# Two transformer blocks on one core: products of constants between a norm and its first matmuls

## The chip, the cores and the metric

The kernel runs on one core of a Trainium2 chip. A core has five engines, each with its own instruction queue: TensorE (PE) multiplies 128x128 tiles and writes PSUM, VectorE (DVE), ScalarE (ACT) and GpSimd (POOL) do the rest of the arithmetic, and SyncE (SP) issues most of the DMAs. They meet through semaphores. The metric is the device time of one execution in microseconds. The kernel before takes 2858.25 us, the median of 3 runs (2855.25 to 2858.81).

## The reference, cut to what matters

The reference is two layers of a first kind of block (differential attention, then neighbourhood attention, each with a squared-relu MLP and modulated norms), followed by two blocks of a second kind, and a last norm. There are 256 latent and 256 context tokens, of 1024 features.

```python
def rms_norm(x, g):
    xf = x.astype(jnp.float32)
    y = xf * lax.rsqrt(jnp.mean(xf * xf, axis=-1, keepdims=True) + NORM_EPS)
    return (y * g.astype(jnp.float32)).astype(x.dtype)
...
    for i in range(DEPTH):
        mod_l = jnp.split((jax.nn.silu(c) @ w_mod[i] + b_mod[i])[:, None, :], N_MOD, axis=-1)
        h_l = modulate(rms_norm(x, norm1_g[i]), mod_l[0], mod_l[1])
        ...
        x = x + mod_l[2] * y_l
        x = x + mod_l[5] * squared_relu_mlp(modulate(rms_norm(x, norm2_g[i]), mod_l[3], mod_l[4]),
                                            w_mlp1[i], w_mlp2[i])
...
    for l in range(DEPTH):
        x = x + HALF_STEP * swiglu(rms_norm_2(x, ffn1_norm[l]), ffn1_w_gu[l], ffn1_w_down[l])
        x = x + hybrid_mixer(rms_norm_2(x, mix_norm[l]), positions, ...)
        x = x + memory_cross_attention(rms_norm_2(x, ca_norm[l]), rms_norm_2(mem, mem_norm[l]), ca_w_q[l], ca_w_kv[l], ca_w_o[l])
        x = x + HALF_STEP * swiglu(rms_norm_2(x, ffn2_norm[l]), ffn2_w_gu[l], ffn2_w_down[l])
    return rms_norm_2(x, final_norm)
```

All of it is float32. The added products compute nothing of this: their results are not read.

## The kernel before, in words

**Layout.** The residual stream `XT` is held transposed, eight tiles of 128 features by 512 tokens (256 of the context, 256 latents); in the second kind of block, and in the last MLP, only the 256 latent columns count. Weights come by DMA in blocks of up to 1 MB into a ring of three slots. ScalarE makes the rounded copy `Wh` (L1249) and VectorE the remainder `Wl` (L1689); activations are split the same way into `HTh` and `HTl`. `passes` (L685) multiplies such a pair in three passes, each a matmul of one record in the trace. Two split blocks of weights are held at a time.

**A norm.** ScalarE squares the tiles of `XT` into `Pb` and `Lb`. `norm` (L768) lets TensorE multiply the eight squares by a tile of ones, in plain f32, all into one PSUM bank, so that each token's sum stands in every partition. ScalarE makes the inverse root of it (L1280 to L1283), VectorE one Newton step (L1747 to L1749), and then tile by tile VectorE scales (`TMP`, L1760 or L1782), ScalarE rounds (`HTh`) and VectorE takes the remainder (`HTl`, L1767 or L1696). Each `HTl` raises `lo_ready`.

**The first matmuls behind a norm.** `side_by_side` (L739) fills two banks at once, tile by tile, waiting for `lo_ready` at each of the eight tiles. That is a group of 8 x 2 x 3 = 48 matmuls. TensorE has nothing else to do between the norm's last product and the first `HTl`. The last norm, `fin`, is followed by 16 transposes of `HTf`, four into each of four banks, which ScalarE copies out (L1312) for the output's DMA.

**Modulation.** In layer 0, the rows of the modulation are made on TensorE from weights as they land (L800), copied to `modrow`, and 16 products with the constant `fold` (two columns each) turn them into columns. The norm `n1` of layer 0 is issued ahead of the last rows.

**Memory attention.** `attention` (L839) is a loop over units. In step i it issues the scores of unit i, what `behind` gives, the transposes of unit i-2 and the product with the values of unit i-3. For the memory attention, `behind(1)` (in step 2) issues the last 48 matmuls of the queries, and `behind(2)` waits for their copy.

**PSUM and order.** Eight banks of 128x512 f32 are two pools of four, `A` and `V`, each taken in turn. A bank is taken again when the fourth taker before is done with it (`a_free`, `v_free`). The order of each engine's instructions is the order in which its function is written; no scheduler moves anything.

Of the kernel before, what the change touches and what calls it, by code (L numbers as in the profile page):

```python
# [28 lines left out]
P = 128  # L29
# [4 lines left out]
LAT = slice(S, 2 * S)  # L34
ALL = slice(0, 2 * S)
# [38 lines left out]
BANKS = 4  # L74
# [188 lines left out]
def program(nc, I, out):  # L263
    ctx = ExitStack()
    with ctx:

        start = (nc.sbuf_base + 31) // 32 * 32
# [7 lines left out]
        def place(name, shape, dt=F32):  # L275
            t = over(name, shape, here[0], dt)
            here[0] += (4 * int(np.prod(shape[1:])) + 31) // 32 * 32
            assert here[0] <= start + ARENA, name
            return t
# [3 lines left out]
        def sem(name):  # L283
            sems[name] = ctx.enter_context(nc.semaphore(name))
            return sems[name]
# [15 lines left out]
        con = place("con", [P, PACK.shape[1]])  # L301
# [30 lines left out]
        def squares(k):  # L332

            return Pb[:, k, :] if k < 6 else Lb[:, k - 6, :]

        def C(name):
            a, n = CONST[name]
            return con[:, a:a + n]
# [69 lines left out]
        v_full, v_free = sem("v_full"), sem("v_free")  # L408
        A, V = Pool(pa, a_full, a_free), Pool(pv, v_full, v_free)
# [238 lines left out]
        def _(pe):  # L648
# [3 lines left out]
            def mm(o, lhsT, rhs, start, stop, full=None):  # L652
                m = nc.tensor.matmul(o, lhsT=lhsT, rhs=rhs, start=start, stop=stop)  # L653
                if full is not None:
                    m.then_inc(full, 1)

            def turn(o, x, full=None):
                m = nc.tensor.transpose(o, x, C("ident"))  # L658
                if full is not None:
                    m.then_inc(full, 1)  # L660
# [42 lines left out]
            def group(pool, key, o, pairs):  # L703

                if pool.taken():
                    pe.wait_ge(pool.free, pool.taken())
                bank = pool.take(key)
                for i, (a, b, ready) in enumerate(pairs):
                    if ready is not None:
                        ready()  # L710
                    last = i == len(pairs) - 1
                    mm(o(bank), a, b, i == 0, last, pool.full if last else None)
# [52 lines left out]
            X_TOKS = [(X_AT, t) for t in range(2)]  # L765
            CTX_TOKS = [slice(t * P, (t + 1) * P) for t in range(2)]

            def norm(key, tcols):  # L768
                N = tcols.stop - tcols.start
                group(A, key, lambda b: b[:, 0:N],  # L770
                      [(C("ones")[:, 0:P], squares(k)[:, 0:N], lambda: pe.wait_ge(sq_ready, seen.more(sq_ready)))
                       for k in range(KT)])

            def turn_in(key, tok, tiles):
                for k in range(KT):
                    if V.taken():
                        pe.wait_ge(v_free, V.taken())
                    b = V.take((key, k))
                    for t in range(tiles):
                        turn(b[:, t * P:(t + 1) * P], tok[:, t, k * P:(k + 1) * P], v_full if t == tiles - 1 else None)  # L780

            def turn_rows(key, rows):

                if V.taken():
                    pe.wait_ge(v_free, V.taken())
                n = rows.shape[0]
                m = nc.tensor.transpose(V.take(key)[:, 0:n], rows, C("ident")[0:n, 0:n])
                m.then_inc(v_full, 1)

            def condition_rows(pool, key):  # L790

                w = raw_slot()
                if pool.taken():
                    pe.wait_ge(pool.free, pool.taken())
                b = pool.take(key)
                for k in range(KT):
                    j = k % 4
                    m = nc.tensor.matmul(b[32 * j:32 * j + 32, 0:256], lhsT=cT[:, k, :], rhs=w[:, k, :],  # L800
                                         start=k < 4, stop=k >= 4)
                m.then_inc(pool.full, 1)
                used(pool, key)

            def modulation(i):
                pe.wait_ge(v_free, V.nth("cond"))
                for n in range(FIRST_MOD):
                    condition_rows(V, ("modr", i, n))
                    if n == X_AFTER:
                        pe.wait_ge(const_in, 16)  # L810
                        pe.wait_ge(rows_in, ROW_LOADS * 16)
                        for j in range(2):
                            turn_rows(("rows", j), rowt[0:min(P, N_ROWS - j * P), j, :])
                        pe.wait_ge(tok_in, 4 * 16)
                        turn_in("x", xtok, 4)
                    if n == X_AFTER + 3:
                        norm(("n1", i), ALL)
                if V.taken():
                    pe.wait_ge(v_free, V.taken())
                b = V.take(("mod", i))  # L820
                pe.wait_ge(v_free, V.nth(("modr", i, FIRST_MOD - 1)))
                for n in range(2 * KT):
                    mm(b[:, 2 * n:2 * n + 2], modrow[:, n // 2, n % 2 * P:n % 2 * P + P], C("fold"), True, True,
                       v_full if n == 2 * KT - 1 else None)

            def next_modulation(n):

# [11 lines left out]
            def attention(tag, kind, todo, scores, values, dv, o_rows, also=lambda i: None, behind=lambda i: None):  # L839


                for i in range(len(todo) + 3):
                    if i < len(todo):
                        for m in range(2 if kind == "diff" else 1):
                            pairs = scores(*todo[i], m)
                            if V.taken():
                                pe.wait_ge(v_free, V.taken())
                            b = V.take((tag, "S", i, m))
                            for j, (q, k, *where) in enumerate(pairs):
                                last = j == len(pairs) - 1  # L850
                                mm(b[:, where[0] if where else slice(0, todo[i][2])], q, k, j == 0, last,
                                   v_full if last else None)
                    if i:
                        behind(i - 1)
                    if 0 <= i - 2 < len(todo):
                        u = i - 2
                        n = todo[u][2] // P
                        pe.wait_ge(pn_ready, seen.more(pn_ready))
                        if A.taken():
                            pe.wait_ge(a_free, A.taken())  # L860
                        b = A.take((tag, "T", u))
                        src = Pb[:, u % 3 * 2, :]
                        for t in range(n):
                            turn(b[:, t * P:(t + 1) * P], src[:, t * P:(t + 1) * P], a_full if t == n - 1 else None)
                    if i >= 3:
                        u = i - 3
                        h, qt, nk = todo[u]
                        pe.wait_ge(a_free, A.nth((tag, "T", u)))
                        r = o_rows(h)
                        group(V, (tag, "O", u), lambda b: b[r, 0:P],  # L870
                              [(values(h, t), PT[:, u % 2, t * P:(t + 1) * P], None) for t in range(nk // P)])
                    also(i)
                behind(len(todo) + 2)
# [40 lines left out]
            def first_layer(i):  # L914
                if i == 0:
                    modulation(0)
                else:
                    norm(("n1", i), ALL)
                tiles = qk_tiles(i)
                order = len(tiles)  # L920
                for j in range(order + 2):
                    if j < order:
# [4 lines left out]
                        n = c.stop - c.start  # L927
# [10 lines left out]
                    if 0 <= j - 1 < order:  # L938
                        c = tiles[j - 1][1]
                        n = c.stop - c.start  # L940
# [13 lines left out]
                if i == 0:  # L954
# [18 lines left out]
                    N, tc = 512, ALL  # L973
                    src = ht(ALL)
                else:
# [4 lines left out]
                    N, tc = S, LAT  # L980
                    src = quarters(lambda k: O_AT["near"] + k)
                for n in range(4):
                    linear(V, ("o", i), 2 * n, (0, P), src, N, n == 0 and i == 0)
                norm(("n2", i), tc)
                for c in range(FF1 // P // CHUNK + 1):
                    if i == DEPTH - 1 and c == MEMORY_CHUNK:
                        pe.wait_ge(mem_in, 16)
# [62 lines left out]
                group(V, (tag, j, "r"), lambda b: b[:, 0:S], [(C("halves"), x, None)])  # L1050

            def mixer(l):
                norm(("mix", l), LAT)
                for n in range(3):
                    linear(A, ("fqk", l), 2 * n, (0, P), hx, S, n == 0)
                section_values(("fv", l))
# [17 lines left out]
                for j, offsets in enumerate(((0, P), (0, HEAD), (0, P))):  # L1074
                    linear(A, (("sb", l), "qk"), 2 * j, offsets, hx, S)
                    if j == 0:
# [3 lines left out]
                        b = V.take(("cum", l))  # L1080
# [121 lines left out]
            for i in range(DEPTH):  # L1202
                first_layer(i)
            for l in range(DEPTH):
# [1 line left out]
                mixer(l)  # L1206
                cross(l)
                ffn(l, 2)
            norm(("fin",), LAT)
            pe.wait_ge(h_ready, seen.more(h_ready, KT))  # L1210
            for t in range(2):
                for half in range(2):
                    if A.taken():
                        pe.wait_ge(a_free, A.taken())
                    b = A.take(("out", t, half))
# [1106 lines left out]
```

## Time and profile before

| | us |
|---|---|
| median of 3 runs | 2858.25 |
| lowest, highest | 2855.25, 2858.81 |
| the profiled execution | 2857.25 |
| its span (first to last instruction) | 2855.4 |
| TensorE busy | 2686.0 |
| VectorE busy | 1726.7 |
| ScalarE busy | 1283.4 |

Times come from one profiled execution. "PE" rows are matmuls and transposes, "PEld" their weight loads, which run beside them. A duration of a matmul's record holds its drain, so consecutive records overlap; the pace is the distance of two starts. The granted clock is the share of TensorE's full 2.4 GHz; it has two levels, 0.5 and 1, and a value between is a mean over a stretch. A wait in square brackets is the idle time of the engine before that instruction, with what ended it. "issue" there means that the profile shows nothing that it waited for.

### The profile page before, as it was taken

What the parts mean: (1) busy time and instruction counts of PE and PEld (TensorE: products, weight loads), DVE (VectorE), ACT (ScalarE), POOL (GpSimd) and SP (SyncE); (2) the same over time, 40 slices, a digit from 0 to 9 for tenths busy, and PEclk for the clock granted to TensorE, in tenths of its full rate; (3) what the DMA queues carried; (4) which work ended last, traced back from release to release, by engine and by line L of the source; (5) the groups of instructions that cost most, each with busy time, mean ns of one, the idle gap of its engine ahead of it and who ended that gap; (6) DMA issues with size and microseconds to landing.
All of it is one profiled execution on the core that took longest, in us unless ns stands there. A gap on an engine that the chain in (4) does not pass through costs nothing.

```text
span 2855.4 us, 45577 instructions
## 1 busy us (share of the span) xinstructions
PE 2686.0 (94%) x18789; PEld 2397.7 (84%) x18789; DVE 1726.7 (60%) x3256; ACT 1283.4 (45%) x2348; POOL 129.6 (5%) x146
## 2 busy tenths in 40 slices
PE   5999989999979889999989989899999999898998
PEld 3777567888868589999989879899999998798998
DVE  4554855454565566676555767676665447675763
ACT  3544733223254554454443445554544434455543
POOL 1000000000040410000000020000000000110000
PEclk9999999999989899999999999999999999999999
DMA  7555532323252335556544314365665543243654
GB/s 246 192 177 172 169 103 74 104 91 101 99 108 76 73 96 172 163 173 181 167 154 139 117 52 159 115 177 163 192 182 168 168 142 111 67 141 119 175 165 119
DMA packets 511518, 397.09 MB, mean 139 GB/s; under 512 B 21848, under 2 KB 487008, under 8 KB 511184
## 3 DMA queue, kind: packets, MB, share of 16 engines
q1 hardware_dynamic: 508512, 387.10, 44.7%
q0 software_dynamic: 2080, 3.53, 1.0%
q8 instruction: 150, 2.46, 0.4%
q10 hardware_dynamic: 720, 3.54, 0.3%
q14 instruction: 56, 0.46, 0.1%
HBM read 393.08 MB, written 1.05 MB: 138 GB/s over the span
## 4 chain that ended last, share of the span: by engine, by line
PE 83%; DVE 9%; ACT 4%; issue 1%; DMA 1%; POOL 1%; SPq 0%; DVEq 0%; ACTq 0%
PE pv L688 42%; PE pa L688 31%; PE pv L653 5%; PE pa L653 3%; DVE Wl L1689 2%; ACT Wh L1249 2%; PE pa L658 1%; PE pa L800 1%; DMA ring<-in_w_mod_dram 1%; DVE Lb L1827 1%; POOL Pb L2244 0%; DVE TMP L1782 0%; DVE T L1748 0%; DVE TMP L1760 0%; DVE HTl L1767 0%
## 5 line engine op out<-in xcount | busy, mean ns | idle before, releaser
L1689 DVE TENSOR_TENSOR Wl<-ring,Wh 128x1024 fp32r<-128x1024 f32 (+3 forms) x688 | 765.2, 1153 | 351.3 <-ACT Wh L1249 348.7
L1249 ACT ACTIVATE Wh<-ring 128x1024 fp32r<-128x1024 f32 (+3 forms) x688 | 647.4, 990 | 504.9 <-PE pv L688 502.0
L688 PE MATMUL pa<-HTl,Wh 128*128 128x256 f32 (+1 forms) x1648 | 539.5, 327 | 43.9 <-DVE HTl L1767 26.9
L688 PE MATMUL pv<-HTl,Wh 128*128 128x256 f32 (+1 forms) x1872 | 545.9, 292 | 9.1 <-DVE XT L1807 2.2
L688 PE MATMUL pv<-HTh,Wl 128*128 128x256 f32 (+1 forms) x1872 | 537.0, 287 | 0.0
L688 PE MATMUL pv<-HTh,Wh 128*128 128x256 f32 (+1 forms) x1872 | 536.6, 287 | 0.0
L688 PE MATMUL pa<-HTh,Wl 128*128 128x256 f32 (+1 forms) x1648 | 524.1, 318 | 0.0
L688 PE MATMUL pa<-HTh,Wh 128*128 128x256 f32 (+1 forms) x1648 | 523.7, 318 | 0.0
L688 PEld LDWEIGHTS pa<-HTl,Wh 128*128 128x128 f32 x1648 | 324.2, 197 | 79.8 <-issue 43.3
L688 PEld LDWEIGHTS pv<-HTl,Wh 128*128 128x128 f32 x1872 | 358.9, 192 | 22.5 <-issue 7.4
L688 PEld LDWEIGHTS pv<-HTh,Wl 128*128 128x128 f32 x1872 | 359.2, 192 | 3.2 <-issue 0.5
L688 PEld LDWEIGHTS pv<-HTh,Wh 128*128 128x128 f32 x1872 | 359.1, 192 | 2.7
L688 PEld LDWEIGHTS pa<-HTh,Wl 128*128 128x128 f32 x1648 | 324.5, 197 | 19.7 <-issue 1.4
L688 PEld LDWEIGHTS pa<-HTh,Wh 128*128 128x128 f32 x1648 | 323.7, 196 | 18.5
L1312 ACT ACTIVATE BIG<-pa 128x256 f32<-128x256 f32 (+1 forms) x206 | 78.7, 387 | 331.3 <-PE pa L688 323.4
L688 PE MATMUL pv<-HID2l,Wh 128*128 128x256 f32 x704 | 199.2, 283 | 0.0
L688 PE MATMUL pv<-HID2h,Wl 128*128 128x256 f32 x704 | 199.2, 283 | 0.0
L688 PE MATMUL pv<-HID2h,Wh 128*128 128x256 f32 x704 | 199.2, 283 | 0.0
L688 PE MATMUL pv<-HID1l,Wh 128*128 128x512 f32 (+1 forms) x512 | 172.0, 336 | 0.0
L688 PE MATMUL pv<-HID1h,Wl 128*128 128x512 f32 (+1 forms) x512 | 172.0, 336 | 0.0
L688 PE MATMUL pv<-HID1h,Wh 128*128 128x512 f32 (+1 forms) x512 | 172.0, 336 | 0.0
L1797 DVE SCALAR_TENSOR_TENSOR XT<-pv,MOD,XT 128x256 f32<-128x256 f32 x216 | 95.6, 479 | 114.9 <-PE pv L688 114.1
(223 smaller groups left out, 4052.4 us busy)
## 6 DMA issues: line engine op xcount, KB each, us to landing
ring<-in_ffn_w_gu_dram SPq DMA_DIRECT2D x176, 512.0 KB, 5.0
ring<-in_w_mlp_dram SPq DMA_DIRECT2D x64, 1024.0 KB, 5.3
ring<-in_w_in_dram SPq DMA_DIRECT2D x54, 1024.0 KB, 5.1
ring<-in_w_mod_dram SPq DMA_DIRECT2D x48, 1024.0 KB, 5.6
ring<-in_ffn_w_down_dram SPq DMA_DIRECT2D x64, 704.0 KB, 4.5
ring<-in_a_w_qkv_dram SPq DMA_DIRECT2D x12, 1024.0 KB, 5.2
ring<-in_b_w_qkv_dram SPq DMA_DIRECT2D x12, 1024.0 KB, 5.2
ring<-in_w_out_dram SPq DMA_DIRECT2D x8, 1024.0 KB, 5.0
```

What stands on the lines that cost most here:

```text
L653: m = nc.tensor.matmul(o, lhsT=lhsT, rhs=rhs, start=start, stop=stop)
L658: m = nc.tensor.transpose(o, x, C("ident"))
L688: m = nc.tensor.matmul(o, lhsT=x, rhs=y, start=first and j == 0, stop=last and j == 2)
L800: m = nc.tensor.matmul(b[32 * j:32 * j + 32, 0:256], lhsT=cT[:, k, :], rhs=w[:, k, :], start=k < 4, stop=k >= 4)
L1249: ins = nc.scalar.activation(Wh[rows, p % SPLIT, a:b], ring[rows, i % RING, a:b], ACT.Copy)
L1312: nc.scalar.activation(dst, src(b), func, scale=scale).then_inc(a_free, 1)
L1689: ins = v.tensor_tensor(Wl[rows, p % SPLIT, a:b], ring[rows, i % RING, a:b], Wh[rows, p % SPLIT, a:b].bitcast(F32), ALU.subtract)
L1797: m = v.scalar_tensor_tensor(XT[:, k, half], b[:, at:at + S], MOD[:, i, gate * KT + k, w:w + 1], XT[:, k, half], ALU.mult, ALU.add)
L1827: v.tensor_tensor_reduce(Lb[:, i % 2 * 2 + m, 0:n], b[:, 0:n], mask(*todo[i]), -scale, -NEG, ALU.add, ALU.min, nm[:, i % 2, m:m + 1]).then ...
```

## The change

A new function `keep_busy(pool, n)` issues n plain f32 products of constants, the tile of ones by the first 512 columns of the packed constants `con`, into the bank that the pool gives next, without taking it. It waits first until that bank is free. The taker that follows writes the same bank, on the same engine. There are 92 such products: 5 ahead of the products with `fold`, 7 behind them, 15 behind the norm `n1` of layer 1, 15 and 8 behind `n2` of layers 0 and 1, 8 behind `mix` of each of the two later blocks, 7 in step 2 of each memory attention ahead of the first transposes, and 12 behind the last norm. The norms of the MLPs of the second kind (`f`), of the memory (`nm`) and `ca` get none.

```diff
--- before.py
+++ after.py
@@ -765,11 +765,23 @@
             X_TOKS = [(X_AT, t) for t in range(2)]
             CTX_TOKS = [slice(t * P, (t + 1) * P) for t in range(2)]
 
-            def norm(key, tcols):
+            def keep_busy(pool, n):
+
+
+
+                if pool.taken():
+                    pe.wait_ge(pool.free, pool.taken())
+                b = pool.banks[pool.n % BANKS]
+                for _ in range(n):
+                    nc.tensor.matmul(b[:, 0:512], lhsT=C("ones")[:, 0:P], rhs=con[:, 0:512], start=True, stop=True)
+
+            def norm(key, tcols, busy=0):
                 N = tcols.stop - tcols.start
                 group(A, key, lambda b: b[:, 0:N],
                       [(C("ones")[:, 0:P], squares(k)[:, 0:N], lambda: pe.wait_ge(sq_ready, seen.more(sq_ready)))
                        for k in range(KT)])
+                if busy:
+                    keep_busy(A, busy)
 
             def turn_in(key, tok, tiles):
                 for k in range(KT):
@@ -815,13 +827,13 @@
                         turn_in("x", xtok, 4)
                     if n == X_AFTER + 3:
                         norm(("n1", i), ALL)
-                if V.taken():
-                    pe.wait_ge(v_free, V.taken())
+                keep_busy(V, 5)
                 b = V.take(("mod", i))
                 pe.wait_ge(v_free, V.nth(("modr", i, FIRST_MOD - 1)))
                 for n in range(2 * KT):
                     mm(b[:, 2 * n:2 * n + 2], modrow[:, n // 2, n % 2 * P:n % 2 * P + P], C("fold"), True, True,
                        v_full if n == 2 * KT - 1 else None)
+                keep_busy(A, 7)
 
             def next_modulation(n):
 
@@ -852,6 +864,8 @@
                                    v_full if last else None)
                     if i:
                         behind(i - 1)
+                    if kind == "mem" and i == 2:
+                        keep_busy(A, 7)
                     if 0 <= i - 2 < len(todo):
                         u = i - 2
                         n = todo[u][2] // P
@@ -915,7 +929,7 @@
                 if i == 0:
                     modulation(0)
                 else:
-                    norm(("n1", i), ALL)
+                    norm(("n1", i), ALL, 15)
                 tiles = qk_tiles(i)
                 order = len(tiles)
                 for j in range(order + 2):
@@ -981,7 +995,7 @@
                     src = quarters(lambda k: O_AT["near"] + k)
                 for n in range(4):
                     linear(V, ("o", i), 2 * n, (0, P), src, N, n == 0 and i == 0)
-                norm(("n2", i), tc)
+                norm(("n2", i), tc, 15 if i == 0 else 8)
                 for c in range(FF1 // P // CHUNK + 1):
                     if i == DEPTH - 1 and c == MEMORY_CHUNK:
                         pe.wait_ge(mem_in, 16)
@@ -1050,7 +1064,7 @@
                 group(V, (tag, j, "r"), lambda b: b[:, 0:S], [(C("halves"), x, None)])
 
             def mixer(l):
-                norm(("mix", l), LAT)
+                norm(("mix", l), LAT, 8)
                 for n in range(3):
                     linear(A, ("fqk", l), 2 * n, (0, P), hx, S, n == 0)
                 section_values(("fv", l))
@@ -1206,7 +1220,7 @@
                 mixer(l)
                 cross(l)
                 ffn(l, 2)
-            norm(("fin",), LAT)
+            norm(("fin",), LAT, 12)
             pe.wait_ge(h_ready, seen.more(h_ready, KT))
             for t in range(2):
                 for half in range(2):
```

TensorE at the norm `n2` of layer 0: `Pb`, `Lb` are the squares, `HTl` and `HTh` the operand, `Wh` and `Wl` the weights.

```order
 L653 MATMUL pa<-Pb,con 128x512 [waits sq_ready] x5
 L653 MATMUL pa<-Lb,con 128x512 [waits sq_ready] x2
+L776 MATMUL pa<-con 128x512 [waits a_free]
+L776 MATMUL pa<-con 128x512 x14
 L688 MATMUL pa<-HTl,Wh 128x512 [waits a_free,lo_ready,w_split]
 L688 MATMUL pa<-HTh,Wl 128x512
```

The 15 products stand between the norm's last product and the first of the group of 48. The norms `n1` of layer 1, `n2` of layer 1 and `mix` read the same, with their own counts, and the last norm too, with transposes behind.

TensorE at the end of the modulation of layer 0; `pv<-con,BIG` are the products with `fold`.

```order
+L776 MATMUL pv<-con 128x512 [waits v_free]
+L776 MATMUL pv<-con 128x512 x4
 L653 MATMUL pv<-con,BIG 128x2 [waits v_free]
 L653 MATMUL pv<-con,BIG 128x2 x15
+L776 MATMUL pa<-con 128x512 x7
 L688 MATMUL pa<-HTl,Wh 128x512 [waits lo_ready,w_split]
 L688 MATMUL pa<-HTh,Wl 128x512
```

Five products are ahead of the 16 with `fold`, and the wait for a free bank of `V` is now theirs; seven in a bank of `A` are behind. The lines of the functions below moved by 12, and no other instruction of TensorE did.

TensorE in step 2 of a memory attention, behind the last matmuls of the queries; `pa<-con,Pb` are the transposes of the first unit.

```order
 L688 MATMUL pa<-HTh,Wl 128x256
 L688 MATMUL pa<-HTh,Wh 128x256
+L776 MATMUL pa<-con 128x512 [waits a_free]
+L776 MATMUL pa<-con 128x512 x6
 L658 MATMUL pa<-con,Pb 128x128 [waits a_free,pn_ready]
 L658 MATMUL pa<-con,Pb 128x128
```

Seven products stand ahead of the transposes of unit 0, and so of the scores of unit 3 too. The instructions of ScalarE, VectorE, GpSimd and SyncE are the same, in the same order.

## Rows read from the trace of the kernel before

**Rows 1.** The page: busy time by engine, and the granted clock in 40 slices.

```profile
PE 2686.0 (94%) x18789; PEld 2397.7 (84%) x18789; DVE 1726.7 (60%) x3256; ACT 1283.4 (45%) x2348; POOL 129.6 (5%) x146
...
PEclk9999999999989899999999999999999999999999
```

**Rows 2.** Timeline of TensorE: start, duration, instruction, idle time before it.

```profile
48.86 4.82 PE L653 MATMUL pv<-con,BIG 128*128 128x2 f32 x32 [2.74 <-DVE BIG L1671]
57.44 0.77 PE L688 MATMUL pa<-HTl,Wh 128*128 128x512 f32 x1 [3.76 <-DVE HTl L1767]
...
437.92 0.76 PE L688 MATMUL pa<-HTl,Wh 128*128 128x512 f32 x1 [6.91 <-DVE HTl L1767]
...
803.86 0.55 PE L688 MATMUL pa<-HTl,Wh 128*128 128x256 f32 x1 [6.98 <-DVE HTl L1767]
...
1050.81 0.55 PE L688 MATMUL pa<-HTl,Wh 128*128 128x256 f32 x1 [4.28 <-DVE HTl L1767]
...
1822.10 0.38 PE L658 MATMUL pa<-con,Pb 128*128 128x128 f32 x2
...
1826.93 0.66 PE L658 MATMUL pa<-con,Pb 128*128 128x128 f32 x2 [4.02 <-issue]
...
2247.89 0.55 PE L688 MATMUL pa<-HTl,Wh 128*128 128x256 f32 x1 [4.13 <-DVE HTl L1696]
...
2846.84 3.55 PE L658 MATMUL pa<-con,HTf 128*128 128x128 f32 x16 [5.91 <-DVE HTf L2215]
```

**Rows 3.** Sums by stretch, TensorE: stretch, length, busy (count), clock, DMA share, GB/s.

```profile
57.44:70.45 13.01, 13.01 (x48) 0.85 0.11 36
437.92:451.64 13.72, 13.72 (x49) 0.79 0.00 1
803.86:820.26 16.40, 11.26 (x48) 0.60 0.24 18
1050.81:1058.35 7.54, 7.54 (x49) 0.74 0.00 0
2247.89:2255.86 7.97, 7.97 (x48) 0.69 0.00 0
53.60:57.40 3.80, 0.08 (x1) 0.50 1.10 350
1833.00:1839.00 6.00, 5.10 (x32) 1.00 0.00 0
```

**Rows 4.** Timeline, the last records of the norm `n2` of layer 0.

```profile
429.13 1.88 PE L653 MATMUL pa<-Lb,con 128*128 128x512 f32 x4
```

**Rows 5.** Timeline, passes at full clock, and VectorE's last operands of two groups.

```profile
448.28 0.88 DVE L1767 SCALAR_TENSOR_TENSOR HTl<-TMP,MOD,HTh 128x256 fp32r<-128x256 f32 x2 [0.26 <-ACT HTh L1290]
...
1056.07 0.28 PE L688 MATMUL pa<-HTh,Wh 128*128 128x256 f32 x1
1056.19 0.28 PE L688 MATMUL pa<-HTl,Wh 128*128 128x256 f32 x1
...
1056.41 0.48 DVE L1767 SCALAR_TENSOR_TENSOR HTl<-TMP,MOD,HTh 128x256 fp32r<-128x256 f32 x1 [0.25 <-ACT HTh L1290]
```

**Rows 6.** TensorE's wait from 1458 to 1470 us (total, times, longest).

```profile
PE pa L688 <- DVE Wl L1689: 3.0, 1, 3.0
```

**Rows 7.** Timeline of VectorE in the first memory attention, scores taken up.

```profile
1826.74 0.42 DVE L1827 CUSTOM_DVE_ANT_0 Lb<-pv,con 128x256 f32<-128x256 f32 x1
...
1833.42 0.42 DVE L1827 CUSTOM_DVE_ANT_0 Lb<-pv,con 128x256 f32<-128x256 f32 x1
...
1834.76 0.41 DVE L1827 CUSTOM_DVE_ANT_0 Lb<-pv,con 128x256 f32<-128x256 f32 x1
```

**Rows 8.** Timeline of ScalarE: the copies of the last transposes.

```profile
2847.99 0.60 ACT L1312 ACTIVATE BIG<-pa 128x512 f32<-128x512 f32 x1 [5.88 <-PE pa L658]
...
2849.69 1.33 ACT L1312 ACTIVATE BIG<-pa 128x512 f32<-128x512 f32 x2 [0.26 <-PE pa L658]
```

## The prediction

> **What bounds the kernel now.** I read the page first: TensorE is busy for 94% of the span, and the row of its granted clock shows full speed nearly everywhere, with a dip here and there [rows 1]. So a gap on TensorE is on the path almost wherever it stands. The waits in the timeline come next [rows 2]. Ten gaps belong to the change: one ahead of the products with `fold` and one behind them (2.74 and 3.76 us), one behind each of the norms `n2` of layer 0, `n1` of layer 1, `n2` of layer 1 and `mix` of both blocks, one in each of the two memory attentions, one ahead of the last transposes, all of 2.7 to 7.0 us. (The `mix` of the first block and the second memory attention look like the row of their twin, and only that one stands.) The third view is the sums by stretch [rows 3]: the 48 products that follow such a gap had 0.60 to 0.85 of the clock. A mean of 0.79 over 13.72 us is 5.8 us at the half clock (1.2 GHz). The change wants that time back by giving TensorE work in the gap. Two questions decide: do the added products fit in the gap, and was the cold clock what the stretch behind it waited for?
>
> **What one added product costs.** It is plain f32, 128x128 by 128x512, which is what the norms issue over both token halves. The program has two such products on `Lb` in a norm, and the trace has four records for them, 1.88 us together [rows 4], the last with its drain. A record lasts 0.59 us and the pace is 0.43 us, so the drain is 0.16 us and a product takes 2 x 0.43 = 0.86 us at the full clock, 1.71 at half. Hence 15, 12, 8, 7 and 5 products take 12.9, 10.3, 6.9, 6.0 and 4.3 us. No gap is that long. The work in them waits for nothing but a bank freed long ago, so they start when the gap does (start of the wait's row, less the wait, less the drain of 0.16). Each then ends behind the operand it was to cover. This is what I go by.
>
> The Trainium skill has a rule that speaks otherwise: "TensorE: Matmul & The Clock Gate", section "Back-to-back issue gap", gives N/2.4 + 2.5 ns at the full clock, 216 ns for N = 512. By it 15 products would take 3.2 us and every gap would hold its own. The trace's record alone is twice that and there are two to a product; the measurement decides.
>
> **Place by place.** TensorE's late start is partly paid back, since it then runs at 2.4 GHz. A pass of 256 columns comes every 0.12 us there [rows 5], the group of 48 takes 5.8 us. With 512 columns it takes 13.72 x 0.79 = 10.8 to 13.01 x 0.85 = 11.1 us of full clock [rows 3]; I take 10.9. "Before" below is the end of the group's stretch in [rows 3].
> - `n2` of layer 0, 15 products: from 437.92 - 6.91 - 0.16 = 430.85 to 443.7, group to 454.6; before 451.64. +2.95 us. Behind it the clock is full and TensorE busy for four slices and more [rows 1], so this stays.
> - `n2` of layer 1, 8: from 1046.37 to 1053.25, group to 1059.0; before 1058.35. +0.65.
> - `mix` of block 1, 8: from 2243.6 to 2250.45, group to 2256.2; before 2255.86. +0.35. In block 0 the same +0.65 as in layer 1 goes into a wait of 3.0 us for `Wl` [rows 6] that hangs on VectorE's tables for the angles, not on TensorE: 0, and +0.65 if that cover is thinner than it looks.
> - `n1` of layer 1, 15: from 796.7 to 809.6. But this group follows VectorE: 16.40 us for 11.26 us of work [rows 3]. Four operands wait by 809.6; they take 2.9 us, and TensorE meets VectorE again at the fifth. The end may come at full clock instead of half, 0 to 1.8 us sooner; the group itself leaves too little work there to be sure. I take -0.4.
> - modulation, 5 and 7: the five start at 48.86 - 2.74 - 0.16 = 45.96 and end at 50.25, 1.4 us after the operand. The 32 records of `fold` took 4.82 us, the clock falling on the way [rows 2]; at the full clock throughout they take between half of it and all of it, I say 3.6, and end at 53.8, about where they do now. The seven find a clock that has just had only those tiny products behind it. Here it was 0.50 in this gap [rows 3]. I let it fall some 0.8 us into the seven and come back after 4 us of dense work, as it did in the group behind this gap (0.85 over 13.01 us is 3.9 us at half): 0.9 of a product at full clock, 1.9 in 3.2 us at half, 4.2 more at full, end 61.4; the group ends at 72.3, before 70.45: +1.9. Bounds: all at full clock 59.8, group at 70.7, +0.3; all at half 65.8, group at 76.7, +6.
> - memory attention, 7, twice: they stand ahead of the first pair of transposes, at 1822.10 [rows 2], and end at 1828.1. Behind them in TensorE's order are these (0.2 us) and the fourth scores (0.4 us and the drain), which VectorE can take up at 1828.95 instead of 1826.74 [rows 7]. From there VectorE sets the pace, about 1.34 us a unit (1833.42 to 1834.76), and the fourth unit later is at 1834.4 instead of 1834.76. So the clock kept gives back a late start and 0.3 us more: -0.3 each. Bounds +0.5 (1.5 us a unit) and -1.2.
> - last transposes, 12: from 2840.77 to 2851.05, where the transposes began at 2846.84. Then they are at full clock and ScalarE's copies (0.60 us each [rows 8]) set the pace: first copy at 2851.7, last one done at 2854.1 or a little sooner. Before: 2851.0. +3.0 (2.6 to 3.1), straight into the output.
>
> Sum: 2.95 + 0.65 + 0.35 - 0.4 + 1.9 - 0.6 + 3.0 = +7.9 us. The profiled execution took 2857.25 us (span 2855.4), which gives 2865.2; the median of the runs is 1.0 higher: **2866 us**. With all bounds at one end the sum is +2.6, at the other +14.7. The other engines' instructions are the same and in the same order; where TensorE is late they are late with it.
>
> **Rivals.**
> 1. *The products fit* (faster). If a product cost one record, 0.43 us, 15 would end at 437.3, before the operand at 437.92, and so at every place; the price at which this turns is the gap over the count, 0.46 us for `n2` of layer 0. Gains are then bounded by VectorE: the last `HTl` of layer 0 is done at 449.16 [rows 5], so the group can't end before 450.7: -1.0. Layer 1: last `HTl` 1056.9 [rows 5], end 1057.7: -0.65; `mix` of block 1 about -1.0 by the same pace. Attention: the fourth scores at 1826.74 and four units of 1.34 give 1832.1 and some 0.4 of start-up, -2.2 each; last transposes 1.0. In all -8.1: 2850 us. For: the gaps exceed count x 0.43 each time by a little. Against: the same form of product in [rows 4].
> 2. *The late start is all paid back elsewhere*: +2.6, 2861 us, no change that can be told. It needs the modulation's seven at full clock, the `n1` of layer 1 warm to its end, and both attentions at their best bound. For: a dense TensorE keeps its clock. Against: the three largest terms (2.95, 3.0, 0.65) don't depend on it.
> 3. *The clock doesn't survive the transposes*. Then both attentions run as now, at half clock, but start 1.8 us later (1828.75 for 1826.93 at the second transpose): +1.5 each in place of -0.3, 2870 us. For: nothing in the rows; against: the same loop kept 1.00 from 1833 to 1839 us, transposes included [rows 3]. The Trainium skill, "TensorE: Matmul & The Clock Gate", section "Part 4: PE-mode transpose", says that a transpose doesn't count as busy for the clock; by it this rival would be the likelier one, if the products between the transposes didn't hold the clock alone.
>
> **How the numbers follow.** Forecast 0.54, rival 1 0.15, rival 2 0.25, rival 3 0.06. About 0.2% (5.7 us) is what a measurement of this kernel can tell from no change: slower is the forecast and rival 3, 0.60; same 0.25; faster 0.15. The forecast's own range is 2862 to 2873. The range for 8 times in 10 goes down to take in most of rival 2 and leaves rival 1 out: 2855 to 2873.
>
> **What would show it.** In the changed profile: two records of 128x512 on `con` for each added product, 184 in all, 0.43 us apart; the wait for `HTl` gone and the first product of the group some 6 us later than the operand at layer 0, 2.5 us later at the others; the clock at 1.00 in all these groups but for the modulation's seven and the `n1` of layer 1; the group of `n2` of layer 0 in 10.9 us in place of 13.72; the last transposes some 4 us later against the last `HTf`. Wrong: one record for a product, or a gain that stands after the attention; a stretch where VectorE's or ScalarE's work hid the late start would make the sum smaller.

## The result, and the profile after

| | before | after |
|---|---|---|
| median, timed side by side | 2858.53 us (20 runs) | 2862.92 us (20 runs) |
| ratio of after to before | | 1.0021 (95%: 1.0014 to 1.0027) |
| span of the profiled execution | 2855.4 | 2857.9 |
| TensorE busy | 2686.0 | 2740.1 |

The change costs 6.0 us by the ratio (4.0 to 7.7); the two medians are 4.4 us apart. The forecast was 2866.0, with slower by over 0.2% as the likeliest outcome; the measurement is 0.21% slower, and its interval reaches below 0.2%.

The page of the kernel after, busy time by engine and the granted clock in 40 slices:

```profile
PE 2740.1 (96%) x18973; PEld 2410.1 (84%) x18973; DVE 1726.9 (60%) x3256; ACT 1284.3 (45%) x2348; POOL 130.2 (5%) x146
...
PEclk9999999999999899999999999999999999899999
```

Beside [rows 1]: TensorE has 184 records and 54.1 us more, two records for each of the 92 products, and the other engines have the same work. The clock's row hides the rest in its tenths. Scanned in steps of half a microsecond, TensorE has 174 us at half clock in the kernel before and 96 us in the one after. So 78 us of half clock are gone, and the kernel is slower.

The timeline of TensorE after, at the ten places (start, duration, instruction, idle time before it):

```profile
49.45 3.63 PE L653 MATMUL pv<-con,BIG 128*128 128x2 f32 x32
52.94 6.25 PE L776 MATMUL pa<-con 128*128 128x512 f32 x14
58.63 0.79 PE L688 MATMUL pa<-HTl,Wh 128*128 128x512 f32 x1
...
428.57 13.04 PE L776 MATMUL pa<-con 128*128 128x512 f32 x30
441.04 0.79 PE L688 MATMUL pa<-HTl,Wh 128*128 128x512 f32 x1
...
797.42 13.04 PE L776 MATMUL pa<-con 128*128 128x512 f32 x30
814.82 0.39 PE L688 MATMUL pa<-HTl,Wh 128*128 128x256 f32 x1 [0.78 <-DVE HTl L1781]
818.29 0.38 PE L688 MATMUL pa<-HTl,Wh 128*128 128x256 f32 x1 [2.49 <-DVE HTl L1781]
...
1046.27 7.03 PE L776 MATMUL pa<-con 128*128 128x512 f32 x16
...
1822.61 6.17 PE L776 MATMUL pa<-con 128*128 128x512 f32 x14
...
2243.66 7.03 PE L776 MATMUL pa<-con 128*128 128x512 f32 x16
...
2840.43 10.46 PE L776 MATMUL pa<-con 128*128 128x512 f32 x24
2850.73 1.91 PE L658 MATMUL pa<-con,HTf 128*128 128x128 f32 x16
```

Against [rows 2]: no operand is waited for where the gaps of 2.7 to 7.0 us were, apart from two waits inside the group of `n1` of layer 1. The 15 products take 13.04 us with the last drain, 0.86 each, where the gap had 6.91. The group of 48 behind them starts at 441.04 instead of 437.92.

The sums by stretch of TensorE after (stretch, length, busy (count), clock, DMA share, GB/s):

```profile
441.04:452.36 11.32, 11.32 (x51) 1.00 0.00 0
1053.10:1058.90 5.80, 5.80 (x50) 1.00 0.00 0
58.63:69.96 11.33, 11.33 (x50) 1.00 0.00 1
2250.50:2256.30 5.80, 5.80 (x50) 1.00 0.00 0
1829.00:1835.00 6.00, 6.00 (x38) 1.00 0.44 126
```

These answer to [rows 3]: four groups, and the stretch of the memory attention. The groups run at the full clock throughout, where they had 0.69 to 0.85. Layer 0 takes 11.32 us instead of 13.72, so 2.4 us of its late start come back and the rest stays.

The two profiles can be laid beside each other instruction by instruction, since VectorE's are the same in both. The start of one in the profile after, less its start in the one before, is the offset; its step over a place is what that place costs. The table has these steps (us), worked out in the same way for all kernels, each against the first profile of the kernel before; minus is sooner. The step at the modulation runs from VectorE's copy of the last row, ahead of the five products, to its first instruction behind the group of 48, and so takes in both gaps, as the forecast does. "Before again" is a second profile of the kernel before, and shows what moves without any change. The columns behind "after" belong to the experiments. Their names are explained there.

| place | forecast | before again | after | after again | 256 columns | half the count | transposes | double |
|---|---|---|---|---|---|---|---|---|
| modulation | +1.9 | +1.45 | +0.5 | +2.5 | +0.5 | +0.15 | +0.55 | +11.1 |
| `n2`, layer 0 | +2.95 | -0.6 | +3.0 | +3.0 | -0.7 | -0.7 | -0.7 | +15.9 |
| `n1`, layer 1 | -0.4 | -0.3 | -0.4 | 0 | -0.2 | +0.15 | +0.15 | +6.6 |
| `n2`, layer 1 | +0.65 | -0.1 | +0.65 | +0.65 | -0.55 | -0.55 | -0.6 | +7.5 |
| `mix`, block 0 | 0 | 0 | -1.5 | -1.5 | +0.7 | +1.1 | +1.1 | +2.8 |
| `mix`, block 1 | +0.35 | 0 | +0.35 | +0.35 | -1.4 | -1.4 | -1.4 | +7.2 |
| memory attentions | -0.6 | 0 | -1.0 | -1.0 | -4.4 | -4.4 | -4.4 | +11.0 |
| last transposes | +3.0 | 0 | +2.75 | +2.75 | -1.4 | -1.4 | -1.4 | +13.05 |
| sum of the places | +7.9 | +0.4 | +4.4 | +6.8 | -7.4 | -7.1 | -6.6 | +75.2 |
| everywhere else | | 0 | -2.0 | -7.7 | -6.0 | +1.6 | +1.1 | +2.9 |
| whole span | | +0.4 | +2.4 | -0.9 | -13.5 | -5.5 | -5.4 | +78.1 |

What is left between two profiles, "everywhere else", is mostly stretches at half clock in dense work that stand in one and not in the other. They are worth 1.5 to 3 us each, of either sign, and two profiles of one kernel differ by them: the two of the changed kernel by 5.7 us. So the offset at the end of a single profile tells less than its steps, and less than the timed medians. The profiled execution after, 2859.67 us, is also the fastest of its 20, and that of the 256 columns, 2843.82 us, the fastest of its 8.

### The profile page after: what moved, and what is told of

Its sections match the earlier page's. It is cut to its first block, busy times and chain, and to the rows that moved or that the text cites. A ratio compares the mean times of both kernels' runs of the same rounds, so it can differ in the third digit from the quotient of the medians.

```text
span 2857.9 us, 45944 instructions
## 1 busy us (share of the span) xinstructions
PE 2740.1 (96%) x18973; PEld 2410.1 (84%) x18973; DVE 1726.9 (60%) x3256; ACT 1284.3 (45%) x2348; POOL 130.2 (5%) x146
## 4 chain that ended last, share of the span: by engine, by line
PE 85%; DVE 8%; ACT 3%; issue 1%; DMA 1%; POOL 1%; SPq 0%; ACTq 0%; DVEq 0%
PE pv L688 41%; PE pa L688 31%; PE pv L653 5%; PE pa L653 3%; DVE Wl L1703 2%; PE pa L776 2%; ACT Wh L1263 2%; PE pa L812 1%; PE pa L658 1%; DMA ring<-in_w_mod_dram 1%; DVE Lb L1841 1%; DVE TMP L1796 0%; SPq L2305 0%; DVE HTl L1710 0%; POOL Pb L2258 0%
## 5 line engine op out<-in xcount | busy, mean ns | idle before, releaser
L688 PE MATMUL pa<-HTl,Wh 128*128 128x256 f32 (+1 forms) x1648 | 533.7, 324 | 11.1 <-DVE Wl L1703 5.9
L688 PE MATMUL pa<-HTh,Wl 128*128 128x256 f32 (+1 forms) x1648 | 518.1, 314 | 0.0
L688 PE MATMUL pa<-HTh,Wh 128*128 128x256 f32 (+1 forms) x1648 | 517.9, 314 | 0.0
L688 PEld LDWEIGHTS pa<-HTh,Wl 128*128 128x128 f32 x1648 | 318.5, 193 | 20.7 <-issue 2.9
```

The source lines that it names most:

```text
L688: m = nc.tensor.matmul(o, lhsT=x, rhs=y, start=first and j == 0, stop=last and j == 2)
```

## The experiments

In the texts below, theory A is that of the prediction: only the time of the products against the gap decides, a late start is paid in full where TensorE sets the end, and a kept clock is worth no more than the other engines' pace allows. B and C in the first four texts are its rivals there; in the last four the rivals of each are named in its text.

**The same products with 256 columns** (label fit256).

```diff
-                    nc.tensor.matmul(b[:, 0:512], lhsT=C("ones")[:, 0:P], rhs=con[:, 0:512], start=True, stop=True)
+                    nc.tensor.matmul(b[:, 0:256], lhsT=C("ones")[:, 0:P], rhs=con[:, 0:256], start=True, stop=True)
```

> Same places and counts, but each product has 256 moving columns in place of 512, so it should cost 0.43 us instead of 0.86. Theory A (late starts): every wait for the operand comes back as a short one (0.3 to 0.8 us), TensorE starts each group when its operand is there, at the full clock, and VectorE's pace bounds the gain. Against the kernel before: n2 of layer 0 -1.0, n2 of layer 1 -0.65, mix of block 1 -1.0 to -1.5, memory attentions -2.2 each, last transposes -1.0, together about -8 us, 2850 us. Theory B (a kept clock is given back at another place, as dips that move): no difference from the kernel before within 2 us, and as much time at the half clock elsewhere. Theory C (the cost of the change is TensorE's use of banks or of SBUF against the other engines, not its own time): half of the change's loss stays, +3 us.

Measured: 2851.19 us, ratio to before 0.9969 (0.9958 to 0.9980), -8.9 us (5.7 to 12.0 faster). The timeline of TensorE at `n2` of layer 0:

```profile
428.73 6.64 PE L776 MATMUL pa<-con 128*128 128x256 f32 x30
...
435.82 0.47 PE L688 MATMUL pa<-HTl,Wh 128*128 128x512 f32 x1 [0.45 <-DVE HTl L1781]
```

The 15 products end 0.45 us ahead of the operand, and the first pass takes 0.47 us instead of 0.76 in [rows 2], since the clock is full. The number of records, the places and the bank are those of the changed kernel; only the time of one record is halved. That turns +6 us into -9, so theory B (no difference beyond 2 us) and theory C (half of the loss stays) fall. The gain of 0.7 us at this norm is less than the 1.0 expected; that at the last transposes, 1.4, is more.

**Twice the products** (label double).

```diff
-                for _ in range(n):
+                for _ in range(2 * n):
```

> Twice the counts of the changed kernel (10, 14, 30, 30, 16, 16, 14, 16, 14, 24 products of 512 columns). Theory A: each added product is 0.857 us of late start, paid in full wherever the changed kernel was already late and in part where VectorE set the end. Against the changed kernel: modulation +10, n1 of layer 1 +8, n2 of layer 0 +12.9, n2 of layer 1 +6.9, mix +4.5 and +6.9, attentions +6 each, last transposes +10.3: about +71 us, near 2934 us. Theory B (dips that move): the products themselves are covered and the loss stays some us: 2866 to 2875.

Measured: 2937.43 us, ratio to before 1.0269 (1.0251 to 1.0287); 74.5 us above the changed kernel, for 92 more products of 0.86 us, 78.9 us in all. Theory B (2866 to 2875 us) falls. The steps sum to 70.8 us more than in the changed kernel, for the 71 of theory A. Here even the places that cost nothing in the changed kernel pay: `n1` of layer 1 6.6 us and `mix` of block 0 2.8. At `n2` of layer 0 the 15 further products cost all of their 12.9 us; at `n1` of layer 1 they cost 7.0, because VectorE's cover over TensorE's lateness takes up the first 5.9.

**Transposes in place of products** (label turns), four of 128 columns for each.

```diff
-                    nc.tensor.matmul(b[:, 0:512], lhsT=C("ones")[:, 0:P], rhs=con[:, 0:512], start=True, stop=True)
+                    for t in range(4):
+                        nc.tensor.transpose(b[:, t * P:(t + 1) * P], con[:, 0:P], C("ident"))
```

> Each added product is replaced by four transposes of the identity (128x128 each) into the same bank, by the pace of 0.11 us in the trace the same 0.45 us as a product of 256 columns. It fits the gaps. It asks whether transposes hold the clock. If they do (theory A with any TensorE work), the granted clock is 1.00 in the groups behind and the time is that of the kernel with 256 columns, about 2850. If a transpose does not count for the clock, the clock falls in the gaps as before and the time is that of the kernel before, 2858, with the first matmuls of each group at half clock.

Measured: 2851.71 us, ratio 0.9970 (0.9958 to 0.9982). The timeline at `n2` of layer 0, and the sum of the stretch that the transposes fill:

```profile
429.32 6.71 PE L777 MATMUL pa<-con 128*128 128x128 f32 x60
436.40 0.47 PE L688 MATMUL pa<-HTl,Wh 128*128 128x512 f32 x1 [0.37 <-DVE HTl L1782]
```

```profile
429.32:436.03 6.71, 6.71 (x61) 1.00 0.22 82
```

Sixty transposes take 6.71 us and fit, the clock stays at 1.00 over them, and the gain is that of the 256 columns. The Trainium skill, "TensorE: Matmul & The Clock Gate", section "Part 4: PE-mode transpose", says that a transpose doesn't count as busy for the clock in the way a product does; this run disagrees, for f32 transposes with nothing between them: 6.71 us of them at 1.00.

**The kernel before, once more** (label before_again), with no edit.

> The kernel before once more, for a second trace of it. Theory A: the dips of the clock behind the norms and in the memory attentions stand where they stood, since long gaps cause them; the short ones elsewhere (near 225, 1471, 1658 to 1700, 2450 us in the first trace) come and go and move the time by 1 to 2 us each. If instead all dips stand in the same places, the ones that the changed kernel has at 1116, 1143 and 1256 us and the first trace has not are caused by the change.

Measured: 2857.62 us. Stretches at half clock at 1113 and 1140 us are there, which the first profile of before hadn't and the one of after had (+1.5 and +1.7 us). They are not the change's doing. The third of the expectation, at 1256 us, is in neither profile of before, so this run leaves it open. At `n2` of layer 0 this profile is 0.6 us sooner than the first, because the clock came back sooner. So a gain of 0.7 there is within what the kernel before does by itself. At the modulation it loses 1.45 us: the clock fell 0.6 us into the products with `fold` (2.3 us into them in the first profile), and they took 6.37 us instead of 4.82:

```profile
47.49 6.37 PE L653 MATMUL pv<-con,BIG 128*128 128x2 f32 x32 [2.74 <-DVE BIG L1671]
```

A step of 1.5 us at the modulation is therefore within what the kernel before does by itself, too. The steps at the places behind `n2` of layer 1 agree within 0.02 us.

**Half the count, 512 columns** (label half); two of the seven edited lines are shown.

```diff
-                    norm(("n1", i), ALL, 15)
+                    norm(("n1", i), ALL, 7)
...
-                norm(("n2", i), tc, 15 if i == 0 else 8)
+                norm(("n2", i), tc, 7 if i == 0 else 4)
```

> The products as in the changed kernel, plain f32, 512 columns, but half as many of them: 3 and 4 at the modulation, 7 behind n1 of layer 1 and behind n2 of layer 0, 4 behind n2 of layer 1 and behind mix, 3 in each memory attention, 6 ahead of the last transposes. Theory A (only the time of the products against the gap counts; one takes 0.86 us): 3 take 2.6 us, 4 take 3.4, 7 take 6.0, 6 take 5.1, and each ends before its operand. So it reads like the 256 columns with the full counts: 2851 us, about -7.5 against the kernel before, the clock at 1.00 in the groups behind the norms, n2 of layer 0 0.7 us earlier than in the kernel before, the last transposes 1.4 earlier. Rival B (the width of the products, not their time, cost something, as a plain f32 product of 512 columns followed by fp32r passes): still slower than the kernel before, by 1 to 3 us.

Measured: 2849.41 us, ratio 0.9970 (0.9957 to 0.9982). At `n2` of layer 0:

```profile
428.96 6.17 PE L776 MATMUL pa<-con 128*128 128x512 f32 x14
...
436.04 0.47 PE L688 MATMUL pa<-HTl,Wh 128*128 128x512 f32 x1 [0.91 <-DVE HTl L1781]
```

Seven products end 0.91 us ahead of the operand. The column in the table is that of the 256 columns within 0.4 us everywhere. The half-clock time is 128 us here and 104 with the 256 columns, for the same gain. The shape of the product costs nothing that shows: rival B falls.

**Only the seven and the last twelve** (label seven_and_last); the other products are gone. One of the edits against the changed kernel:

```diff
-                keep_busy(V, 5)
+                if V.taken():
+                    pe.wait_ge(v_free, V.taken())
```

> The kernel before, and of the added products only the seven behind the products with fold and the twelve ahead of the last transposes. Theory A: last transposes +2.75 as in the changed kernel, whatever stands ahead. At the modulation the question is what kept the clock under the seven, where it was forecast to fall. Theory C (the five products ahead of fold carried it over the tiny products): without them the clock is at half when the seven start, as it is in the gap of the kernel before; they take some 8 us in place of 6, the group of 48 ends 2.0 us later than in the kernel before, and the sum is +4.75 us: 2863.3. Rival D (the seven alone are enough, the gap behind fold was what let the clock fall): the modulation stays at +0.25 to +0.5, the sum is +3.1 us: 2861.6.

Measured: 2862.54 us, ratio 1.0016 (1.0007 to 1.0026), +4.6 us. Its interval is 2.0 to 7.4 us and holds both forecasts, so only the profile can tell them apart. The step at the modulation is +2.3, the one at the last transposes +2.75, 5.1 in all, for the 4.75 of theory C and the 3.1 of rival D. The modulation's timeline, and its sums by stretch:

```profile
53.53 8.42 PE L776 MATMUL pa<-con 128*128 128x512 f32 x14
```

```profile
48.80:53.50 4.70, 4.70 (x32) 0.74 1.10 353
53.53:61.40 7.87, 7.87 (x16) 0.72 0.73 236
61.40:73.00 11.60, 11.60 (x54) 1.00 0.00 0
```

Without the five products the clock falls under those with `fold` (0.74), is low under the seven (0.72), and these take 8.42 us where the changed kernel took 6.25. That favours theory C, though the next run shows that it is not the whole answer. At `n2` of layer 0, where this kernel has no products, its step is -0.7 again.

**The changed kernel, once more** (label after_again), with no edit.

> The changed kernel once more, for a second profile. Theory A: the offsets at the ten places come back within 0.3 us (+3.0 at n2 of layer 0, +0.65 at n2 of layer 1, +0.36 at mix of block 1, +2.75 at the last transposes, 0 to +0.3 at the modulation), while the dips of the clock that stand elsewhere (1116, 1143, 1256, 2320, 2450 us) may stand in other places or be gone. Rival B: those dips come back in the same places, and are part of what the change does.

Measured: 2856.35 us in its one run. That is less than any of the 20 timed executions, because its stretches at half clock elsewhere are fewer (-7.7 us in the table). The steps come back within 0.1 us at every place but two: at `n1` of layer 1 the step is 0, not -0.4, and at the modulation it is +2.5, not +0.5. Its timeline, and its sums by stretch; behind them the same stretches of the first profile after:

```profile
50.02 3.63 PE L653 MATMUL pv<-con,BIG 128*128 128x2 f32 x32
53.51 7.95 PE L776 MATMUL pa<-con 128*128 128x512 f32 x14
60.89 0.80 PE L688 MATMUL pa<-HTl,Wh 128*128 128x512 f32 x1
```

```profile
50.00:53.50 3.50, 3.50 (x33) 1.00 0.97 305
53.50:60.90 7.40, 7.40 (x17) 0.77 0.71 236
```

```profile
49.45:52.90 3.45, 3.45 (x33) 1.00 1.10 349
52.94:58.60 5.66, 5.66 (x15) 1.00 0.94 301
```

`fold` runs at 1.00 in both. Then, with the same instructions in the same order, the clock stays at 1.00 under the seven in one execution and averages 0.77 in the other. The expectation was missed here (0 to +0.3, behind the products with `fold`, where the step is +1.9). The half-clock stretches at 1116, 1143 and 1256 us, on the other hand, came back, as rival B said, and so did the one at 2320; the one at 2450 is shorter. The first two also stand in the second profile of before, and all three in those of half the count, of the transposes and of the doubled count, but none in that of the 256 columns. What places them isn't settled.

**256 columns at chosen places** (label chosen): none at the modulation and at `n1` of layer 1, but 16 in the near attention of layer 1.

```diff
+                            if s == 3 and m == 1 and tag[-1] == 1:
+                                keep_busy(A, 16)
                             ready = pn_ready if m else dv_ready
```

> The products with 256 columns, in full counts, only where they moved the end: n2 of both layers, mix of both blocks, the memory attentions, the last transposes; none at the modulation and behind n1 of layer 1; and 16 more in the near attention of layer 1, in the gap of 7.6 us ahead of the transposes that wait for GpSimd's Pb. Theory A (a kept clock is worth what the maker of the operands lets TensorE take): the ones left out were worth nothing, and the near attention behind its gap follows VectorE and GpSimd, so 0 to -2 us from the 16; in all 2850 us, -7 to -10 against the kernel before. Rival: the clock kept in the near attention and behind it gives back all the time at half clock there (some 17 us at half from 948 to 970 us), that is -8 us more: 2843.

Measured: 2849.24 us, ratio 0.9965 (0.9953 to 0.9977), -10 us (6.6 to 13.4 faster). It is the lowest ratio, but its interval holds the ratios of the three others that fit (0.9969, 0.9970, 0.9970). The timeline of TensorE at the near attention, and the sum of the stretch behind it; the last fence is the kernel before over the matching stretch:

```profile
958.62 7.29 PE L776 MATMUL pa<-con 128*128 128x256 f32 x32
966.37 0.66 PE L658 MATMUL pa<-con,Pb 128*128 128x128 f32 x4 [0.46 <-POOL Pb L2260]
```

```profile
966.40:981.00 14.60, 13.98 (x126) 1.00 0.26 46
```

```profile
967.00:981.50 14.50, 14.30 (x108) 0.80 0.27 44
```

The clock goes from 0.80 to 1.00 and the same time holds 126 records in place of 108. The step over the near attention is -2.75 us, where it is -0.1 with the 256 columns, without these 16, and -1.4 with half the count, -1.2 with the transposes and -1.2 in seven_and_last, whose half-clock stretches fell differently. So the 16 brought 1.3 to 2.7 us by the one comparison or the other: about the 2 that theory A allowed at most, or a little more, and far from the rival's 8.

## Why the prediction was right

**The price of a product was right, and it decided the sign.** Two records of 0.43 us: the rows after have 30 records in 13.04 us, less the last drain 0.86 us a product. The products outlast every gap, which the 256 columns and half the count show from the other side. Rival 1 was the right account of what fitting products do. Its 2850 us stands against 2849.4 to 2851.7 in the three kernels whose products fit (256 columns, half the count, transposes), but it rested on a price that this form doesn't have. The Trainium skill, "FP8 and Floating Point Precision", section "TensorE Precision Notes", says that true FP32 takes four passes through the array. Four times the 216 ns of the formula in the prediction is, as an estimate, 0.86 us, and the trace agrees with 0.86.

**Where TensorE sets the end, the late start was paid as worked out.** `n2` of layer 0: +2.95 forecast, +3.0 in both profiles. Layer 1 +0.65 and +0.65, `mix` of block 1 +0.35 and +0.35. Here only the late start and the passes of 0.23 and 0.12 us were needed.

**Last transposes, +3.0 against +2.75.** The products did end where expected, and ScalarE's copies set the pace. I had counted four copies at 0.60 us each, 2.4 us:

```profile
2851.37 2.06 ACT L1326 ACTIVATE BIG<-pa 128x512 f32<-128x512 f32 x4 [9.59 <-PE pa L658]
```

All four take 2.06 us, with no wait between them, since one starts before the last has ended; in [rows 8] the four took 3.03 us. The 0.3 us are the miss.

**Memory attention, -0.3 each against -0.46 and -0.52.** VectorE takes the fourth scores at 1829.48, which less the offset of 0.51 ahead of this place is 1828.97, for 1828.95 in the working:

```profile
1829.48 0.42 DVE L1841 CUSTOM_DVE_ANT_0 Lb<-pv,con 128x256 f32<-128x256 f32 x1 [2.13 <-PE pv L653]
1830.82 0.41 DVE L1841 CUSTOM_DVE_ANT_0 Lb<-pv,con 128x256 f32<-128x256 f32 x1
...
1833.48 0.41 DVE L1841 CUSTOM_DVE_ANT_0 Lb<-pv,con 128x256 f32<-128x256 f32 x1
1834.82 0.41 DVE L1841 CUSTOM_DVE_ANT_0 Lb<-pv,con 128x256 f32<-128x256 f32 x1
```

Four units of 1.335 us lead to 1834.82, 1834.31 less the offset, against 1834.76 in [rows 7]. The pace was right, and the difference is a slip of the working: 1828.95 and four times 1.34 are 1834.3, not 1834.4, which is -0.45, and by the same sum its upper bound (1.5 us a unit) is +0.2, not +0.5. Rival 3 falls: the clock is at 1.00 from 1829 to 1835 us, transposes included.

**`n1` of layer 1, -0.4 against -0.4 and 0.** TensorE meets VectorE again inside the group (waits of 0.78 and 2.49 us in the rows after), as the working said, and the group ends with VectorE. That the size was met in one profile says little: the second profile of the kernel before has -0.3 here with no change. So the gain that I put at the end of the group isn't shown.

**`mix` of block 0, 0 against -1.5: missed.** The cover by `Wl` held, so the late start cost nothing. But behind the wait for `Wl` the kernel before had the half clock once more, from 1471 to 1475 us, and this is gone in both profiles after. I had not looked behind the wait. TensorE's row behind this wait, in the kernel before, after, and with the 256 columns:

```profile
1469.90 0.39 PE L688 MATMUL pa<-HTl,Wh 128*128 128x256 f32 x1 [3.02 <-DVE Wl L1689]
1475.08 0.39 PE L688 MATMUL pa<-HTl,Wh 128*128 128x256 f32 x1 [2.36 <-DVE Wl L1703]
1466.23 0.58 PE L688 MATMUL pa<-HTl,Wh 128*128 128x256 f32 x1 [4.13 <-DVE Wl L1703]
```

The operand `Wl` comes at VectorE's time, so a group that ends later leaves TensorE a shorter wait. The late start of 0.65 us cut it from 3.02 to 2.36 us, and no half clock followed, in both profiles. In the kernels whose products fit the group ends sooner and the wait is 4.1 us: the clock falls within it and stays low about twice as long (1464 to 1471 us with the 256 columns, 1469 to 1476 with half the count), which costs 0.7 to 1.1 us. That the wait decides is a reading of these profiles; no run changed the wait alone.

**Modulation, +1.9 against +0.5 in one profile and +2.5 in the other: the step that was taken for settled and isn't.** The working let the clock fall some 0.8 us into the seven, after the tiny products with `fold`. One execution did close to that, with 7.95 us for the seven; the other kept the full clock and came near the lower bound of +0.3. The forecast should have been two cases, not one with bounds, and the kernel before alone moves by 1.45 us here. The five products ahead do matter for `fold`: its products took 3.63 to 3.98 us in the six profiles that have work ahead of them, and 4.82 to 6.37 us in the four that have none.

The places sum to +4.4 and +6.8 us in the two profiles, and the timed comparison gives +6.0 (4.0 to 7.7). Of the 3.5 us between +7.9 and +4.4, `mix` of block 0 is 1.5, the modulation 1.4, the attentions 0.4 and the end 0.25. In the second profile the modulation is 0.6 above its forecast and `n1` 0.4, and the sum is 1.1 us short. The match with the timed +6.0 is not proof of the whole sum. The steps say nothing of the stretches at half clock elsewhere, which the timed runs hold too, and both profiled executions were faster than the other 19 that were timed, with -2.0 and -7.7 us elsewhere. What is shown is the cost place by place. Rival 2, no change that can be told, was not far off: 2861 us against 2862.92.

## What to carry to other kernels

Work that is to keep the clock has a budget, the gap that it fills, and its cost is read from a record of the same form and type; plain f32 with 512 columns cost 0.86 us, and half of it turned the sign of the change. What it can bring is bounded by the engine that makes the operands, not by the time at half clock: 78 us less of it went with +6 us where the products outlasted the gaps, and with products that fit (72 us less, 48 with half the count) the kernel was 9 us faster. Where the work is too long already, each further product costs in full if TensorE sets the end, and nothing up to the slack if the maker of the operand does, as the doubled counts showed.

## What the runs showed of the hardware

- The clock is not a function of the program alone. The seven products of the modulation had 1.00 in one execution and 0.77 in another, with the same instructions in the same order, and one kernel's profiles differ in several stretches at half clock, each worth 1.5 to 3 us.
- Plain f32 transposes of 128x128 alone held the clock at 1.00 for 6.7 us (429.32 to 436.03 us of the run with transposes), and came every 0.11 us.
- Filling one gap changes the next fall of the clock. Behind `mix` of block 0 TensorE's next wait was 3.0 us in the kernel before, with one stretch at half clock behind it; 2.4 us in the changed kernel, with none; and 4.1 us in the kernels whose products fit, with a stretch about twice as long.
